# Two sides of a recurrent branch, five steps apart instead of abreast

## The reference, cut to what matters

```
def step(state, inp):
    r_t, d_t, k_t, v_t, a_t, b_t = inp
    sa = jnp.einsum('bhvk,bhk->bhv', state, a_t)
    state = (state * d_t[:, :, None, :] + sa[..., None] * b_t[:, :, None, :]
             + v_t[..., None] * k_t[:, :, None, :])
    return state, jnp.einsum('bhvk,bhk->bhv', state, r_t)
```

## Time and profile before

| | us |
|---|---|
| median of 3 runs | 3988.12 |
| lowest and highest | 3988.08, 3989.89 |
| the profiled execution, device time | 3987.26 |
| its span, first to last instruction | 3986.0 |
| PE busy | 3701.4 (93% of the span) |
| DVE, ACT, POOL busy | 1828.8, 1323.9, 1168.3 |

### The profile page before, as it was taken

How to read it: one execution, slowest core, us unless ns; L and a number is a source line. 1 busy time by engine, 2 the same in 40 slices (tenths; PEclk the granted TensorE clock), 3 DMA queues, 4 the chain that set the end, 5 groups by cost and what they waited for, 6 DMA issues and landing times.

```text
span 3986.0 us, 44685 instructions
## 1 busy us (share of the span) xinstructions
PE 3701.4 (93%) x18366; PEld 3032.3 (76%) x18366; DVE 1828.8 (46%) x2404; ACT 1323.9 (33%) x2153; POOL 1168.3 (29%) x624
## 2 busy tenths in 40 slices
PE   5898898979888899999999898999988999999998
PEld 4786887868866677888888776777666778888886
DVE  3435444444167544323322453897542444343435
ACT  3323232232344333122122344775122233232222
POOL 3322313231100232333333212665133323232321
PEclk8988898988999999999999999999999999999999
DMA  3201010000100352111111123222354431111111
GB/s 116 58 1 54 1 39 27 19 29 10 48 12 1 110 163 88 51 46 52 48 48 48 64 90 101 74 83 87 99 159 144 137 95 48 48 48 48 48 48 53
DMA packets 282073, 253.62 MB, mean 64 GB/s; under 512 B 11333, under 2 KB 221569, under 8 KB 281872
## 3 DMA queue, kind: packets, MB, share of 16 engines
q1 hardware_dynamic: 267264, 216.52, 18.1%
q10 hardware_dynamic: 11520, 25.17, 1.7%
q0 software_dynamic: 3088, 9.10, 0.6%
HBM read 214.04 MB, written 36.70 MB: 63 GB/s over the span
## 4 chain that ended last, share of the span: by engine, by line


## 5 line engine op out<-in xcount | busy, mean ns | idle before, releaser
L401 POOL TENSOR_TENSOR weight_lo<-stage,weight_hi 128x1024 fp32r<-128x1024 f32 (+4 forms) x265 | 631.5, 2387 | 1488.7 <-ACT weight_hi L393 1461.2
L364 PE MATMUL psum<-hT_hi,weight_hi 128*128 128x512 f32 x2240 | 893.0, 399 | 13.2 <-ACT sig_g L744 6.6
L365 PE MATMUL psum<-hT_lo,weight_hi 128*128 128x512 f32 x2240 | 879.8, 393 | 0.0
L366 PE MATMUL psum<-hT_hi,weight_lo 128*128 128x512 f32 x2240 | 878.9, 392 | 0.0
L364 PEld LDWEIGHTS psum<-hT_hi,weight_hi 128*128 128x128 f32 x2240 | 426.4, 190 | 111.7 <-issue 13.9
L365 PEld LDWEIGHTS psum<-hT_lo,weight_hi 128*128 128x128 f32 x2240 | 426.0, 190 | 93.4 <-issue 5.8
L366 PEld LDWEIGHTS psum<-hT_hi,weight_lo 128*128 128x128 f32 x2240 | 425.3, 190 | 89.8
L393 ACT ACTIVATE weight_hi<-stage 128x1024 fp32r<-128x1024 f32 (+4 forms) x329 | 315.9, 975 | 466.9 <-PE psum L366 406.4
L1931 DVE TENSOR_TENSOR x<-x,psum 128x512 f32<-128x512 f32 x432 | 290.0, 687 | 215.2 <-PE psum L366 214.6
L364 PE MATMUL psum<-weight_hi,act_hi 128*128 128x512 f32 x864 | 339.0, 392 | 0.0
L366 PE MATMUL psum<-weight_hi,act_lo 128*128 128x512 f32 x864 | 338.7, 392 | 0.0
(11 more groups left out here) (369 smaller groups left out, 5898.5 us busy)
## 6 DMA issues: line engine op xcount, KB each, us to landing
stage<-in_w_in SPq DMA_DIRECT2D x64, 512.0 KB, 4.0
stage<-in_w_up SPq DMA_DIRECT2D x44, 512.0 KB, 3.9
scratch_gates<-gate ACTq DMA_DIRECT2D x64, 256.0 KB, 2.0
gs<-scratch_gates SPq DMA_DIRECT2D x64, 256.0 KB, 2.8
stage<-in_w_out SPq DMA_DIRECT2D x32, 512.0 KB, 4.7
stage<-in_w_ffn_up SPq DMA_DIRECT2D x32, 512.0 KB, 4.1
stage<-in_w_ffn_down SPq DMA_DIRECT2D x32, 512.0 KB, 3.8
stage<-in_w_down SPq DMA_DIRECT2D x22, 512.0 KB, 3.3
```

What stands on the lines that cost most here:

```text
L364: q.matmul(out, stat[0], mov[0], start=first, stop=False)
L365: q.matmul(out, stat[0], mov[1], start=False, stop=False)
L366: return q.matmul(out, stat[1], mov[0], start=False, stop=final)
L401: g.q.tensor_tensor(lo, K.staged(w), hi.bitcast(F32), ALU.subtract).then_inc(*S.w_lo_pool.up(w))
```

## The change

A constant `BATCH_LAG = 5` is added. The pairs of batches are replaced by two chains: side 0 runs batch 0 and then batch 2, side 1 runs batch 1 and then batch 3, with no meeting point between. Side 0 gets five steps ahead; after that each side gets a step in turn until both chains have ended, and so side 1 has its last five steps alone. No instruction, buffer or wait is added or taken away; they only stand in another order. A chain that reaches the end of its first batch goes on inside the same step, so that `state` of batch 0 and the first `gram` of batch 2 are issued together.

```
+BATCH_LAG = 5
...
         o.do("state_zero", blk)
-        for n0 in (0, 2):
-            running = [order_batch(o, blk, n0, 0), order_batch(o, blk, n0 + 1, 1)]
-            while running:
-                running = [g for g in running if next(g, "end") != "end"]
+        sides = [itertools.chain(order_batch(o, blk, side, side), order_batch(o, blk, side + 2, side)) for side in range(2)]
+        advance(sides[0], BATCH_LAG)
+        while sides:
+            sides = [g for g in sides if next(g, "end") != "end"]
         o.handover()
```

## The result

| | before | after |
|---|---|---|
| median, us | 3988.84 (6 runs) | 4035.76 (6 runs) |
| lowest and highest | 3986.65, 3991.32 | 4032.35, 4053.89 |
| profiled execution: device time, span | 3987.26, 3986.0 | 4034.34, 4033.1 |

A forecast was written before the change was run, and what follows sets the result against it. PE was taken to bound the kernel, busy for 93% of the span. Four blocks at 13 us more waits and 1.5 us more low clock add 58 us to 3987.3, giving a 4046 us median, range 4003 to 4085.

The forecast's parts named there:

- The bound: In the recurrence, PE's in-order list makes a block's length; ACT, DVE and POOL gain nothing by being early.
- The waits, plus 13 us a block: PE's waits in a recurrence block: 24.8 us where there were 11.8, mostly before `first` and where one side is alone.
- The 99 us stay: PE's work in a recurrence block at full clock, 99 us of the 124.1, was to stay the same.
- L969 at 0.68: DVE's addition before `first` was to take 0.68 us each time, since POOL's next mask waits for it.
- The levels: Levels of the recurrence: nothing changes, 0.2 us of wait a level as before, 2.5 for the block.
- The clock, plus 1.5 us a block: Loss to PE's low clock in a block: 14.8 us against 13.3, bounds minus 5 to plus 7.
- The sum: Four recurrence blocks, each longer by 13 us of waits and 1.5 of clock: 58 us in all, 4046 us.
- (B): Rival, chance 0.13: the clock stays high in the blocks, about +1 us a block, 3984 to 3996, not slower.
- (C): Rival, chance 0.10: clock low nearly all through starts, ends and both `state`s, 13 + 10 us a block and up, 4075 to 4095.
- (D): Rival, chance 0.07: the other side's matmuls cover the waits before `first`, half the low clock goes, 3935 to 3975 us.

The follow-up runs named there:

- e4: The changed kernel with nine extra 128x128 identity matmuls in front of each `first`, inside its wait: 4045.15 us, ratio 1.0138.
- e3: The changed kernel with two empty steps between `gram` and `first` in every batch but batch 0: 4059.46 us, ratio 1.0170.
- e9: The kernel before with 14 extra identity matmuls before side 0's `first` and three at the head of each `state` chunk: 3964.79 us, ratio 0.9935.

## Why the prediction was right, and by how much

**The bound.** PE's own list bounds the recurrence: right. DVE's busy time fell by 9 us and POOL's by 2, at no gain, and the waits went into the span at their full length.

**The waits, plus 13 us a block.** Right in kind and place, somewhat too large in size. PE waits for L969 16 times instead of 8, as written, for 45.4 us instead of the 50 expected; and at just the places named it waits for ACT and DVE where one side is alone. The forecast counts from start to start, so the hidden 0.2 us belong to each wait that the profile lists: 8.85 + 1.55 = 10.4 us a block. The parts that were too large are those where a side is alone or waits for its own `first`: side 1's `first` at the start took 2.7 us (2.49 listed), not 3.2; side 0's 4.0 (3.83), not 4.3; the end 4.4 (0.69 + 0.83 + 0.78 + 1.31, and four times 0.2), not 4.8. One cause shows: from the end of the last eviction to `first` it is 2.2 us, not 2.4. The rest stays open. The middle's two waits came out as 2.7 and 2.8, where 2.2 and 3.2 were forecast, the same sum.

**The 99 us stay.** Not quite: by the estimate above the list itself grew by 1.8 us a block, which the forecast put at nothing.

**L969 at 0.68.** Right: after, it takes 691 to 694 ns in all 16 places, against 678 to 1735. The row was misread on the way: min, median and max don't say that 15 of the 16 were slow. In the trace side 0's eight take 1.73 us each, begun just behind POOL's second mask, and side 1's eight 0.68. The mask of POOL no longer runs beside it:

```profile
L969 DVE TENSOR_TENSOR TT<-Al,ident x16: 691/692/694, 181.5 to 969.0; 128x512 f32<-128x512 f32 x16
```

**The levels.** Unchanged, as forecast: a level takes 5.57 us (209.80 to 215.37), as in the earlier trace rows, with no wait in it.

**The clock, plus 1.5 us a block.** Wrong in sign, within its bounds of minus 5 to plus 7: the estimate above gives 1.1 us a block less, 10.9 for 12.0, where the forecast had 14.8 for 13.3. The places are as written: low stretches behind the idles before `first` and at the start of a block, and none in `state` of side 0. Read off the first block's rows, the start cost some 4.5 us, not 6, the middle some 6, not 6.6, and the end 0.5, not 2.2. The end was partly luck: in e4 the same steps took 6.8 us longer.

**The sum.** Forecast 13 + 1.5 = 14.5 us a block, measured 11.1: the waits were 2.6 too high and the clock 2.6 too high, and the longer list, not in the sum, gave 1.8 back. So the total is nearer than its parts.

**The rivals.** (B), the clock stays high and the change costs nothing: its premise fails. An idle of 2.5 us doesn't slow the `first` right behind it (rows of 0.63 and 0.66 us), but the low clock comes a microsecond later, with 1.91 us for a correction, and costs some 1.4 us each time. Its sum fails too: with the clock held high by filling, the change still costs 9.5 us a block. (C), low clock all through: e3's first block comes near, 143.8 us at 0.84, so it was no idle thought, but the changed kernel isn't there. (D), the waits are covered: one step of the other side doesn't, and e3 shows that even three steps cover `first` only by uncovering others.

## What to carry to other kernels

When two chains share an in-order engine, running them abreast hides each one's latency behind the other's work at every step; a lag keeps that in the steady part, but leaves one chain alone at each end, and gives every gathering point (here `gram` to `first`) a wait per chain instead of one for both. So count the uncovered answers in the engine's own list, end by end, before hoping for overlap. And after any change of order, compare granted clocks before explaining a few microseconds: where TensorE's work is thin, filling its waits with matmuls that are thrown away took the kernel before down by 0.65%, and no order tried here gained anything by itself.

## What the runs showed of the hardware

- The clock of TensorE fell to 1.2 GHz while PE was busy. In the kernel before, PE is busy for the whole 12.45 us of `state`, with 64-column matmuls, and the granted clock is 0.64 there; it fell at about 229.4, 3.4 us after the last idle, of 0.28 us. With three 128-column matmuls more a chunk, 0.67 us, the blocks of e9 had 0.99 to 1.00, though their list is longer.
- The same thin steps ran at either level. The lone side's last steps took 13.85 us in the changed kernel, at a granted clock of 0.94, and 20.65 us in e4, at 0.50, with the same waits of 0.7 to 1.3 us between the same matmuls. The clock was high in front of them in the one and had just fallen in the other.
- Where VectorE's L969 (both inputs in SBUF) and a mask of POOL meet, the one that starts second is the long one. In the kernel before, an L969 begun 0.07 us behind a mask took 1.73 us (183.18, the mask 1.26), and one begun 0.15 us ahead of a mask took 0.68, and the mask 1.66 (184.84). In the changed kernel they don't meet, and L969 takes 0.69.
- The identical list of a block took 134.7, 138.2, 140.7 or 143.8 us in one execution (e3), by where it fell relative to the clock's falls. A measured difference of under some 10 us a block can't be put down to order alone without this being looked at.
